# Building the gate tables of a PEER expert layer: one comparison for both tables on VectorE, and the gates multiplied in on GpSimd

## The chip, the cores and the metric

The kernel runs on one core of a Trainium2 chip. The metric is the device time of one execution in microseconds (us). An execution has five engines that run side by side and meet at semaphores: TensorE (PE, with its weight loads PEld), VectorE (DVE), ScalarE (ACT), GpSimd (POOL) and SyncE (SP), which here only issues transfers.

## The reference, cut to what matters

The kernel computes two layers of a backbone for 128 context tokens and 512 latent tokens, all in float32. Each layer ends in a PEER expert mixer. Every token has 8 heads, each head picks 16 pairs (i1, i2) of 128 x 128 experts with a softmax gate, so a token has 128 selections:

```python
v1, i1 = lax.top_k(s1, PEER_TOPK)
v2, i2 = lax.top_k(s2, PEER_TOPK)
...
idx = jnp.take_along_axis(cidx, pos, axis=-1)          # i1 * 128 + i2
gates = jax.nn.softmax(best, axis=-1).astype(h.dtype)
...
act = jax.nn.gelu(jnp.einsum('td,ted->te', xb, u_tab[ib])) * gb
return jnp.einsum('te,ted->td', act, v_tab[ib])
```

For three of the five tiles of 128 tokens (384 tokens) the kernel computes this densely over all 16,384 experts, and needs a dense table of gates: for each token a 128 x 128 matrix that holds the gate at (i1, i2) and zero elsewhere.

## The kernel before, in words

The program is a row of stages, each a block with a barrier of all engines at its end: load, modulation, the RWKV and Fourier layer, `peer` for layer 0, the Hyena layer, `peer` for layer 1, store. `peer` itself is `norm_modulate`, `peer_route` (top-16 and gates), `peer_dense_gates` (the change is here), `peer_experts` and `add_and_norm`. Nothing of one stage's engine work runs beside that of another.

`peer_dense_gates` gets `selT`: for each selection (partition) and each of 384 tokens the first index (row 0), the second index (row 1) and the gate (row 2). Tokens go in 96 groups of 4 (`QT`). A group k uses slot `k % 4` of the buffer `hot` and of the PSUM banks 0 to 3. In a slot, `hot[:, u, 1]` holds four one-hot tables of the second index, `hot[:, u, 0]` four one-hot tables of the first index times the gate, each 128 selections x 128 keys.

- VectorE makes table 1 with one `tensor_tensor` of 512 elements per partition (L604, `is_equal` of `selT` row 1 and `iota`), and table 0 with four `tensor_scalar` of 128 (L608), in which the comparison and the product with the gate are one instruction with two per-partition scalars. The 96 groups are written out; from the fifth on, the first instruction of a group waits until TensorE has finished the group four before (`pg_mm`).
- TensorE waits for the tables (`pg_hot`) and for a free bank (`pg_sb`), and does four float32 matmuls of 128x128 (L620), which the trace shows as eight.
- ScalarE copies the bank into `gates_sb`, 512 elements per partition (L632).
- SyncE stores 8,192 KB to memory after each 32 groups (L639), three times. The block ends when the last store has landed.
- GpSimd has no work in this stage but clearing semaphores at its end (L60 to L64).

The order on each engine is the order in the code: there is no planner.

Of the kernel before, what the change touches and what calls it, by code (L numbers as in the profile page):

```python
# [7 lines left out]
ALU = mybir.AluOpType  # L8
# [5 lines left out]
P = 128  # L14
# [52 lines left out]
def sems(ctx, nc, *names):  # L67

    s = {n: ctx.enter_context(nc.semaphore(f"{n}_{nc.next_id()}")) for n in names}
    ctx.callback(clear, nc, s)  # L70
    return s


def buf(ctx, nc, name, *shape, dtype=F32):
    return ctx.enter_context(nc.sbuf_tensor(f"{name}_{nc.next_id()}", list(shape), dtype))
# [275 lines left out]
PH, NKEY, TOPK = 8, 128, 16  # L351
# [232 lines left out]
def peer_dense_gates(nc, m, selT):  # L584


    QT = 4
    TBLS = 4
    GROUPS = TB // QT
    BLOCKS = NDT  # L590
    with ExitStack() as ctx:
        hot = buf(ctx, nc, "hot", P, TBLS, 2, QT, NKEY)
        G = [buf(ctx, nc, f"gates_sb{i}", P, NKEY, TB) for i in range(2)]
        s = sems(ctx, nc, "pg_hot", "pg_mm", "pg_sb", "pg_st0", "pg_st1")
        stored = [s["pg_st0"], s["pg_st1"]]
        table = [P, QT, NKEY]
        with nc.Block() as block:
            @block.vector
            def _(dve):
                for k in range(BLOCKS * GROUPS):  # L600
                    u = k % TBLS
                    if k >= TBLS:
                        dve.wait_ge(s["pg_mm"], k + 1)
                    dve.tensor_tensor(hot[:, u, 1], selT[:, 1, k * QT:(k + 1) * QT].unsqueeze(2).broadcast_to(table),  # L604
                                      m.iota[:, :].unsqueeze(1).broadcast_to(table), ALU.is_equal)
                    for q in range(QT):
                        t = k * QT + q
                        ins = dve.tensor_scalar(hot[:, u, 0, q, :], m.iota[:, :], selT[:, 0, t:t + 1], selT[:, 2, t:t + 1], ALU.is_equal, ALU.mult)  # L608
                    ins.then_inc(s["pg_hot"], 1)

            @block.tensor
            def _(pe):
                pe.sem_inc(s["pg_mm"], TBLS)
                with pe.Fori(0, BLOCKS * GROUPS // TBLS) as r:
                    for u in range(TBLS):
                        k = TBLS * r + u
                        pe.wait_ge(s["pg_hot"], k + 1)
                        pe.wait_ge(s["pg_sb"], k + 1)
                        for q in range(QT):
                            mm = pe.matmul(m.bank[u][:, q * P:(q + 1) * P], hot[:, u, 1, q, :], hot[:, u, 0, q, :], start=True, stop=True)  # L620
                        mm.then_inc(s["pg_mm"], 1)

            @block.scalar
            def _(act):
                act.sem_inc(s["pg_sb"], TBLS)
                for b in range(BLOCKS):
                    if b >= 2:
                        act.wait_ge(stored[b % 2], 16 * (b // 2))
                    with act.Fori(0, GROUPS // TBLS) as r:
                        for u in range(TBLS):  # L630
                            act.wait_ge(s["pg_mm"], TBLS * r + (b * GROUPS + u + 1 + TBLS))
                            act.activation(G[b % 2][:, :, bass.ds(r * 16 + 4 * u, 4)].rearrange("p i t -> p t i"),  # L632
                                           m.bank[u][:, :].rearrange("p (t i) -> p t i", t=4), ACT.Copy).then_inc(s["pg_sb"], 1)

            @block.sync
            def _(sp):
                for b in range(BLOCKS):
                    sp.wait_ge(s["pg_sb"], (b + 1) * GROUPS + TBLS)
                    sp.dma_start(m.gates[:, :, T0 + b * TB:T0 + (b + 1) * TB].rearrange("a i t -> i a t"), G[b % 2][:, :, :]).then_inc(stored[b % 2], 16)  # L639
                for b in range(BLOCKS - 2, BLOCKS):  # L640
                    sp.wait_ge(stored[b % 2], 16 * (b // 2 + 1))
# [215 lines left out]
def peer(nc, m, layer):  # L857
    with ExitStack() as rows:
        R = Shared()
        R.h = buf(rows, nc, "rows_h", P, NSP, D)  # L860
        R.idx = buf(rows, nc, "rows_idx", P, NSP, PH * TOPK, dtype=U32)
        R.gate = buf(rows, nc, "rows_gate", P, NSP, PH * TOPK)
        with ExitStack() as ctx:
            selT = buf(ctx, nc, "selT", P, 3, TD)
            with ExitStack() as inner:
                S = Shared()
                S.wq = buf(inner, nc, "wq", P, SIDES, KD, P)
                S.keys = buf(inner, nc, "keys", P, SIDES, NKEY)
                S.qT = buf(inner, nc, "qT", P, 2, P)
                s = sems(inner, nc, "ps_keys", "ps_w0", "ps_w1", "ps_w2", "ps_w3")  # L870

                def load_queries(sp):
                    for n in range(SIDES):
                        sp.dma_start(S.wq[:, n], m.i["peer_wq"][layer, n]).then_inc(s[f"ps_w{n // 4}"], 16)
                        if n == 0:
                            sp.dma_start(S.keys[:, :, :], m.i["peer_k"][layer]).then_inc(s["ps_keys"], 16)

                norm_modulate(nc, m, layer, 1, prefetch=load_queries)
                peer_route(nc, m, layer, S, s, selT, R)
            peer_dense_gates(nc, m, selT)  # L880
        R.y = buf(rows, nc, "rows_y", P, NSP, D)
        peer_experts(nc, m, layer, R)
        add_and_norm(nc, m, layer, 1, y=lambda t, h: R.y[:, t, h * BANK:(h + 1) * BANK] if t < NSP else m.bank[2 + 2 * (t - NSP) + h][:, :])
# [1195 lines left out]
```

## Time and profile before

| | us |
|---|---|
| median of 3 runs (5609.91 to 5612.98) | 5610.12 |
| the profiled execution | 5610.12 |
| its span in the trace | 5608.3 |
| TensorE busy | 4504.1 (80%) |
| VectorE busy | 3735.5 (67%) |
| GpSimd busy | 1933.1 (34%) |
| ScalarE busy | 1529.2 (27%) |

The span is the time from the first to the last instruction; the rest of the execution's time, 1.8 us, lies around it. Busy time is summed over stages with quite different limits, so the shares say nothing of the stage that is changed; it runs twice, from 2022.5 to 2212.7 us of the span and from 4265.4 to 4455.5 us. Start times are the ones to trust in it: on VectorE the spans of neighbours overlap, since a span begins when the instruction is taken up.

### The profile page before, as it was taken

The page shows a single profiled execution, that of the slowest core. Times are in us where ns is not written, and L with a number is a line of the kernel's source. Part 1 is how long each engine was busy: PE and PEld are TensorE (multiplying, and loading weights), DVE is VectorE, ACT ScalarE, POOL GpSimd, SP SyncE. Part 2 cuts the span into 40 slices and gives each one's busy share as a digit, 9 for nine tenths or more (in the row PEclk, how much of TensorE's full clock was granted, in tenths as well). Part 3 has the DMA queues.
Part 4 walks back from the last instruction along what each step waited for, and adds up shares of the span by engine and source line. Part 5 has one row for each costly group of instructions (what it writes and reads, how often), then busy time and mean ns, then how long its engine had stood idle before and what let it go on. Part 6 is the DMA issues. An engine that isn't in the chain of part 4 may idle for free. (4 is left out here: it accounts for less than half of the span.)

```text
span 5608.3 us, 71780 instructions
## 1 busy us (share of the span) xinstructions
PE 4504.1 (80%) x24898; PEld 3740.3 (67%) x24898; DVE 3735.5 (67%) x7416; ACT 1529.2 (27%) x2454; POOL 1933.1 (34%) x1556
## 2 busy tenths in 40 slices
PE   3678869679678945999999948877894499999995
PEld 0357758558565934999999945433583499999994
DVE  1143453543523986999999973342398699999997
ACT  0122313222121234333333321110123433333332
POOL 0021312313211320566666640000132056666664
PEclk8879879788789978999999979978997899999997
DMA  9110000000011016999999951101101699999995
GB/s 392 43 56 14 2 14 1 14 14 1 2 59 74 1 52 191 400 398 406 404 399 405 403 196 57 49 27 56 77 1 53 185 400 397 406 404 395 407 406 221
DMA packets 382998, 1049.15 MB, mean 187 GB/s; under 512 B 36647, under 2 KB 168999, under 8 KB 376616
## 3 DMA queue, kind: packets, MB, share of 16 engines
q0 software_dynamic: 147456, 536.94, 24.3%
q1 hardware_dynamic: 235368, 509.88, 24.3%
q8 instruction: 111, 1.82, 0.1%
q14 instruction: 63, 0.52, 0.0%
HBM read 990.62 MB, written 56.07 MB: 187 GB/s over the span
## 5 line engine op out<-in xcount | busy, mean ns | idle before, releaser
L728 PE MATMUL bank<-h_parts,u_parts 128*128 128x384 f32 x6144 | 1116.1, 336 | 97.5 <-DVE u_parts L803 97.5
L728 PEld LDWEIGHTS bank<-h_parts,u_parts 128*128 128x128 f32 x6144 | 1082.3, 188 | 117.3 <-issue 97.8
L738 PE MATMUL bank<-v_parts,gg_parts 128*128 128x512 f32 x4608 | 1095.7, 391 | 0.0
L700 POOL DMA_INDIRECT u_rows<-in_u_rows,rows_idx x512 | 697.5, 1362 | 1087.5 <-DVE dots L807 599.0
L738 PEld LDWEIGHTS bank<-v_parts,gg_parts 128*128 128x128 f32 x4608 | 861.2, 188 | 170.6
L813 DVE SCALAR_TENSOR_TENSOR rows_y<-v_rows,row_scale,rows_y 128x1024 f32<-128x1024 f32 x512 | 661.5, 1293 | 29.0 <-DMA v_rows<-in_peer_v,rows_idx 14.6
L706 POOL DMA_INDIRECT v_rows<-in_peer_v,rows_idx x512 | 608.4, 1188 | 168.2 <-issue 149.3
L807 DVE CUSTOM_DVE_ANT_0 u_rows<-u_rows,rows_h 128x1024 f32<-128x1024 f32 x512 | 622.5, 1216 | 0.0
L803 DVE TENSOR_TENSOR u_parts<-hT,u_parts 128x1024 fp32r<-128x1024 f32 x260 | 317.0, 1219 | 69.4 <-ACT u_parts L776 41.5
L1228 POOL TENSOR_TENSOR early<-region,lmask 128x256 f32<-128x256 f32 x300 | 212.3, 729 | 362.2 <-DVE region L1467 199.1
L302 POOL TENSOR_TENSOR x<-x,gb 128x1024 f32<-128x1024 f32 x20 | 46.9, 2346 | 831.6 <-ACT x L295 831.6
L429 PE MATMUL bank<-hT,wq 128*128 128x128 f32 x2560 | 310.5, 275 | 4.5 <-PEq L60 4.5
L842 DVE TENSOR_TENSOR v_parts<-v_in,v_parts 128x1024 fp32r<-128x1024 f32 x256 | 311.7, 1218 | 0.0
L772 ACT ACTIVATE ge<-bank 128x384 f32<-128x384 f32 x256 | 126.1, 493 | 669.8 <-PE bank L728 543.0
L620 PE MATMUL bank<-hot 128*128 128x128 f32 x1536 | 226.2, 292 | 94.8 <-DVE hot L608 94.8
L429 PEld LDWEIGHTS bank<-hT,wq 128*128 128x128 f32 x2560 | 297.9, 192 | 4.9 <-issue 4.9
L779 ACT ACTIVATE gg_parts<-gg 128x384 fp32r<-128x384 f32 x256 | 134.7, 526 | 587.1 <-PE bank L738 481.8
L620 PEld LDWEIGHTS bank<-hot 128*128 128x128 f32 x1536 | 190.9, 196 | 130.5 <-DVE hot L608 130.4
L776 ACT ACTIVATE u_parts<-hT 128x1024 fp32r<-128x1024 f32 x256 | 269.9, 1054 | 0.0
L781 ACT ACTIVATE v_parts<-v_in 128x1024 fp32r<-128x1024 f32 x256 | 268.0, 1047 | 0.0
L1481 DVE TENSOR_TENSOR XT<-XT,bank 128x512 f32<-128x512 f32 x150 | 103.2, 688 | 237.9 <-PE bank L1304 237.9
L608 DVE TENSOR_SCALAR hot<-iota,selT 128x128 f32<-128x128 f32 x768 | 251.1, 540 | 0.0
(302 smaller groups left out, 6584.9 us busy)
## 6 DMA issues: line engine op xcount, KB each, us to landing
hT<-in_peer_u SPq DMA_DIRECT2D x260, 512.0 KB
v_in<-in_peer_v SPq DMA_DIRECT2D x256, 512.0 KB
w_modt<-in_w_mod SPq DMA_DIRECT2D x24, 2048.0 KB
gates<-gates_sb SPq DMA_DIRECT2D x6, 8192.0 KB, 30.4
g_in<-gates SPq DMA_DIRECT2D x256, 192.0 KB
wq<-in_peer_wq SPq DMA_DIRECT2D x32, 512.0 KB, 12.4
w_hy<-in_hy_w_in SPq DMA_DIRECT2D x9, 1536.0 KB, 6.4
w_rkv<-in_w_rkv SPq DMA_DIRECT2D x6, 1536.0 KB, 6.8
```

Source lines behind the costliest of these rows:

```text
L429: mm = pe.matmul(m.bank[n % 2][:, 0:P], S.wq[:, n, k, :], m.hT[:, k, t * P:(t + 1) * P], start=(k == 0), stop=(k == KD - 1))
L620: mm = pe.matmul(m.bank[u][:, q * P:(q + 1) * P], hot[:, u, 1, q, :], hot[:, u, 0, q, :], start=True, stop=True)
L700: pool.indirect_dma_start(ug[n % GR][:, :], None, m.i["u_rows"], bass.IndirectOffsetOnAxis(ap=R.idx[:, n % 2, n // 2:n // 2 + 1], axis=0)) ...
L706: pool.indirect_dma_start(vg[n % GR][:, :], None, v_table, bass.IndirectOffsetOnAxis(ap=R.idx[:, n % 2, n // 2:n // 2 + 1], axis=0)).then_ ...
L728: mm = pe.matmul(m.bank[j % 2][:, 0:TD], us[:, j % 2, a, k, :], hs[:, b, k, :], start=(k == 0 and i == 0), stop=(k == KD - 1 and i == 2))
L738: mm = pe.matmul(yb[t][c][:, :], gs[:, j, a, t * P:(t + 1) * P], vs[:, j % 2, b, c * BANK:(c + 1) * BANK], start=(first and i == 0), stop= ...
L776: act.activation(us[:, j % 2, 0], u_in[:, (j + 2) % 4], ACT.Copy).then_inc(s["pe_uhi"], 1)
L781: act.activation(vs[:, j % 2, 0], v_in[:, j], ACT.Copy).then_inc(s["pe_vhi"], 1)
L803: dve.tensor_tensor(us[:, slot, 1], u_in[:, raw], us[:, slot, 0].bitcast(F32), ALU.subtract).then_inc(s["pe_ulo"], 1)
L807: dve.tensor_tensor_reduce(ug[q % GR][:, :], ug[q % GR][:, :], R.h[:, q % 2, :], 1.0, 0.0, ALU.mult, ALU.add, sd[:, q:q + 1]).then_inc(s[" ...
L813: dve.scalar_tensor_tensor(R.y[:, q % 2, :], vg[q % GR][:, :], sa[:, q:q + 1], R.y[:, q % 2, :], ALU.mult, ALU.add).then_inc(s["pe_axpy"], 1)
L842: dve.tensor_tensor(vs[:, j % 2, 1], v_in[:, j], vs[:, j % 2, 0].bitcast(F32), ALU.subtract).then_inc(s["pe_vlo"], 1)
```

## The change

In each group VectorE makes both one-hot tables with one `tensor_tensor` of 1,024 elements per partition, without the gate. GpSimd then multiplies table 0 by the gate in place, 512 elements per partition, and TensorE waits for GpSimd (`pg_gated`) where it waited for VectorE. Both new loops run over registers (24 turns of four groups), where VectorE's groups were written out.

```diff
-        s = sems(ctx, nc, "pg_hot", "pg_mm", "pg_sb", "pg_st0", "pg_st1")
+        s = sems(ctx, nc, "pg_hot", "pg_gated", "pg_mm", "pg_sb", "pg_st0", "pg_st1")
...
-        table = [P, QT, NKEY]
+        table = [P, 2, QT, NKEY]
...
-                for k in range(BLOCKS * GROUPS):
-                    u = k % TBLS
-                    if k >= TBLS:
+                with dve.Fori(0, BLOCKS * GROUPS // TBLS) as r:
+                    for u in range(TBLS):
+                        k = TBLS * r + u
                         dve.wait_ge(s["pg_mm"], k + 1)
-                    dve.tensor_tensor(hot[:, u, 1], selT[:, 1, k * QT:(k + 1) * QT].unsqueeze(2).broadcast_to(table),
-                                      m.iota[:, :].unsqueeze(1).broadcast_to(table), ALU.is_equal)
-                    for q in range(QT):
-                        t = k * QT + q
-                        ins = dve.tensor_scalar(hot[:, u, 0, q, :], m.iota[:, :], selT[:, 0, t:t + 1], selT[:, 2, t:t + 1], ALU.is_equal, ALU.mult)
-                    ins.then_inc(s["pg_hot"], 1)
+                        dve.tensor_tensor(hot[:, u], selT[:, 0:2, bass.ds(k * QT, QT)].unsqueeze(3).broadcast_to(table),
+                                          m.iota[:, :].unsqueeze(1).unsqueeze(1).broadcast_to(table), ALU.is_equal).then_inc(s["pg_hot"], 1)
+
+            @block.gpsimd
+            def _(pool):
+                with pool.Fori(0, BLOCKS * GROUPS // TBLS) as r:
+                    for u in range(TBLS):
+                        k = TBLS * r + u
+                        pool.wait_ge(s["pg_hot"], k + 1)
+                        pool.tensor_tensor(hot[:, u, 0], hot[:, u, 0], selT[:, 2, bass.ds(k * QT, QT)].unsqueeze(2).broadcast_to([P, QT, NKEY]),
+                                           ALU.mult).then_inc(s["pg_gated"], 1)
...
-                        pe.wait_ge(s["pg_hot"], k + 1)
+                        pe.wait_ge(s["pg_gated"], k + 1)
```

On VectorE, at the start of the stage, this stood in a row before (L598 is the stage's entry; `pg_mm` counts TensorE's finished groups; "128x512" is partitions x elements of the output):

```order
L598 UNCONDITIONAL_BRANCH [waits barrier_Pool_Activation_PE_DVE_SP_release]
L604 TENSOR_TENSOR hot<-selT,iota 128x512
L608 TENSOR_SCALAR hot<-iota,selT 128x128 x4
...
L604 TENSOR_TENSOR hot<-selT,iota 128x512 [waits pg_mm_7442]
L608 TENSOR_SCALAR hot<-iota,selT 128x128 x4
```

and this stands there now, the body of the loop cut after its first group:

```order
L598 UNCONDITIONAL_BRANCH [waits barrier_Pool_Activation_PE_DVE_SP_release]
L600 UNCONDITIONAL_BRANCH
L600 ISA
L604 ISA [waits pg_mm_7443]
L604 TENSOR_TENSOR hot<-selT,iota 128x1024
L603 REGISTER_ALU
```

The four `tensor_scalar` of a group are gone, and the `tensor_tensor` has doubled. On GpSimd, in the same stage, there was nothing between two barriers but the clearing of semaphores (L64), and then the first gather of the next stage:

```order
L61 UNCONDITIONAL_BRANCH [waits barrier_Pool_Activation_PE_DVE_SP_gather]
L64 ISA x5
L60 UNCONDITIONAL_BRANCH
L695 UNCONDITIONAL_BRANCH [waits barrier_Pool_Activation_PE_DVE_SP_gather]
L700 DMA u_rows_8270<-in_u_rows,rows_idx 128x1024
```

Now its loop stands ahead of them (`pg_hot` counts VectorE's finished tables):

```order
L607 UNCONDITIONAL_BRANCH [waits barrier_Pool_Activation_PE_DVE_SP_gather]
L609 UNCONDITIONAL_BRANCH
L609 ISA
L613 ISA [waits pg_hot_7441]
L613 TENSOR_TENSOR hot<-hot,selT 128x512
L612 REGISTER_ALU
```

GpSimd has become a link between VectorE and TensorE, with one instruction per group.

## Rows read from the trace of the kernel before

**Rows 1.** Groups of instructions, 2015 to 2360 us; busy and mean, idle before and releaser.
```profile
L608 DVE TENSOR_SCALAR hot<-iota,selT 128x128 f32<-128x128 f32 x384 | 126.3, 547 | 0.0
L620 PE MATMUL bank<-hot 128*128 128x128 f32 x768 | 113.1, 293 | 47.4 <-DVE hot L608 47.4
L632 ACT ACTIVATE gates_sb<-bank 128x512 f32 x96 | 102.4, 1067 | 58.7 <-PE bank L620 58.6
L604 DVE TENSOR_TENSOR hot<-selT,iota 128x512 f32<-128x512 f32 x96 | 85.4, 890 | 17.0 <-PEq L60 17.0
```

**Rows 2.** Timeline of the stage: start, length in us, engine and line, idle before.
```profile
2022.52 0.69 DVE L604 TENSOR_TENSOR hot<-selT,iota 128x512 f32<-128x512 f32 x1 [16.96 <-PEq L60]
...
2033.89 0.72 DVE L604 TENSOR_TENSOR hot<-selT,iota 128x512 f32<-128x512 f32 x1
2034.06 1.16 PE L620 MATMUL bank<-hot 128*128 128x128 f32 x8 [0.47 <-DVE hot L608]
2034.49 1.14 DVE L608 TENSOR_SCALAR hot<-iota,selT 128x128 f32<-128x128 f32 x4
...
2176.77 1.09 DVE L604 TENSOR_TENSOR hot<-selT,iota 128x512 f32<-128x512 f32 x1
```

**Rows 3.** Engines' busy time in the steady part, then TensorE's granted clock, DMA.
```profile
2032.00:2178.00 146.00, 103.78 (x718) 86.83 (x719) 146.00 (x451) 96.17 (x91) 0.00 (x0) 1.00 0.41 115
```

**Rows 4.** Timeline of the stage's beginning on TensorE and of its end.
```profile
2024.30 7.67 PE L620 MATMUL bank<-hot 128*128 128x128 f32 x40 [4.67 <-DVE hot L608]
...
2181.28 0.37 SPq L639 DMA_DIRECT2D gates<-gates_sb  x1
2212.70 3.42 ACT L756 ACTIVATE h_parts<-hT 128x384 fp32r<-128x384 f32 x8 [31.45 <-PEq L60]
```

**Rows 5.** VectorE comparing 2,048 elements (timeline, routing) and its 1,024-element subtraction (page).
```profile
1996.35 4.49 DVE L577 TENSOR_TENSOR eq<-ab,iota 128x2048 f32<-128x2048 f32 x2
...
L803 DVE TENSOR_TENSOR u_parts<-hT,u_parts 128x1024 fp32r<-128x1024 f32 x260 | 317.0, 1219 | 69.4 <-ACT u_parts L776 41.5
```

**Rows 6.** Groups of instructions on GpSimd, whole span: its products and sums.
```profile
L1228 POOL TENSOR_TENSOR early<-region,lmask 128x256 f32<-128x256 f32 x300 | 212.3, 729 | 362.2 <-DVE region L1467 199.1 <-PE bank L1296 163.0
L510 POOL TENSOR_TENSOR eq<-eq,idxf 128x2048 f32<-128x2048 f32 x20 | 90.0, 4522 | 326.3 <-DVE eq L577 326.3
L302 POOL TENSOR_TENSOR x<-x,gb 128x1024 f32<-128x1024 f32 x20 | 46.9, 2346 | 831.6 <-ACT x L295 831.6
L516 POOL TENSOR_TENSOR eq<-eq 128x512 f32<-128x512 f32 x10 | 10.4, 1041 | 0.8
```

**Rows 7.** One line of VectorE: its six instructions (min/median/max ns), and the timeline around one.
```profile
L537 DVE TENSOR_TENSOR sel<-gatex,norm x6: 291/293/4252, 1946.1 to 4244.1; 128x128 f32<-128x128 f32 x6
...
2000.92 8.99 POOL L510 TENSOR_TENSOR eq<-eq,idxf 128x2048 f32<-128x2048 f32 x2 [19.58 <-DVE eq L577]
2001.31 4.25 DVE L537 TENSOR_TENSOR sel<-gatex,norm 128x128 f32<-128x128 f32 x1
```

**Rows 8.** Timeline of GpSimd in the RWKV stage.
```profile
333.02 1.98 POOL L1213 TENSOR_TENSOR region<-region,rkv 128x640 f32<-128x640 f32 x1
335.08 1.99 POOL L1216 TENSOR_TENSOR bonus<-region 128x640 f32<-128x640 f32 x1
337.15 1.99 POOL L1218 TENSOR_TENSOR bonus<-bonus,rkv 128x640 f32<-128x640 f32 x1
```

**Rows 9.** Timeline of VectorE in that stretch, and a little later with GpSimd idle.
```profile
333.64 2.04 DVE L1452 TENSOR_TENSOR region<-region,early 128x640 f32<-128x640 f32 x1
335.61 2.15 DVE L1456 TENSOR_TENSOR early<-early,kk 128x640 f32<-128x640 f32 x1
337.79 2.04 DVE L1459 TENSOR_TENSOR x<-kk,region 128x640 f32<-128x640 f32 x1
...
348.58 0.82 DVE L1459 TENSOR_TENSOR x<-rkv,region 128x640 f32<-128x640 f32 x1
349.31 0.82 DVE L1460 TENSOR_TENSOR BK<-early,region 128x640 f32<-128x640 f32 x1
```

## The prediction, made before the changed kernel was run

> **What bounds the kernel now.** I read the page's costliest groups for the lines of the changed stage, then the groups of the stage alone, then its timeline, and last every place where GpSimd and VectorE work at once. The stage is bound by VectorE. In the groups of the stage, TensorE's matmuls and ScalarE's copies sit idle for VectorE's L608 and for TensorE, while VectorE's two lines have no idle time but 17.0 us ahead of the first [rows 1]. In the steady part VectorE is busy for all of 146 us, TensorE for 104, ScalarE for 96, GpSimd for nothing [rows 3]. The pace has to be read from starts, as VectorE's spans overlap (the busy times of its two lines would give 2.2 us a group): L604 starts first at 2022.52 and last at 2176.77, which is 95 steps of 1.624 us [rows 2]. Of one step L604 holds 0.60 (2033.89 to 2034.49) and the four L608 hold the other 1.02. TensorE does its eight matmuls in 1.16 us and then waits 0.47 for L608. ScalarE's copy takes 1.07 us [rows 1]. After the last group comes the store of 8 MB, issued at 2181.28; the next stage starts at 2212.70 [rows 4]. The stage occurs twice, with 96 groups each, so each 0.01 us a group is worth 1.92 us.
>
> **The change part by part.**
>
> VectorE's side by itself. Removed are four L608 and one 512-element L604, 1.624 us a group. Added is one comparison of 1,024 elements. The trace has the same operation with 2,048 elements: two of L577 take 4.49 us, so 2.25 each, and half is 1.12. The subtraction L803 of 1,024 elements takes 1.22 with everything in it [rows 5]. Alone, VectorE would need 1.10 to 1.22 us a group.
>
> GpSimd's side by itself. Its product of 512 elements is bounded by rows 6. Below: L516, 512 elements, 1.04 us. Above: from L1228 (256 elements, 0.73) to L302 (1,024 elements, 2.35) an element costs 2.11 ns, so 512 cost 0.73 + 256 x 2.11 ns = 1.27. A quarter of L510, the same product with one operand spread out, is 1.13. So 1.04 to 1.27.
>
> Each is well below 1.624. If they ran side by side the stage would get shorter. Whether they do is the question on which the sign hangs, and the trace has an answer in two places.
>
> The first is L537, a VectorE product of 128 elements with both inputs in SBUF. Its median is 0.293 us and its longest 4.252. One of the long ones starts at 2001.31, while GpSimd's L510 runs from 2000.92; the first of the two takes 4.52 [rows 6], so it ends at 2005.44, and L537 ends at 2005.56 [rows 7]. VectorE had stood still until GpSimd let go. The second is a stretch of the RWKV stage, where both engines have several 640-element `tensor_tensor` in a row. With GpSimd idle, VectorE starts one such each 0.73 us (348.58, 349.31). Beside GpSimd, its three start at 333.64, 335.61 and 337.79, 2.07 us apart on average [rows 9], and GpSimd's three start at 333.02, 335.08 and 337.15, also 2.07 apart [rows 8]. They alternate: VectorE's end at 335.68, 337.76 and 339.83, each 0.68 or 0.69 us after GpSimd's (335.00, 337.07, 339.14), which is about the work of 640 elements; and GpSimd's end 1.39 and 1.38 us after VectorE's. So 0.69 + 1.38 = 2.07: two `tensor_tensor` that read SBUF cost the sum of the two, not the larger. The new stage is just that pair, 96 times over.
>
> Scaled by elements: VectorE 0.69 x 1024/640 = 1.10 us, GpSimd 1.38 x 512/640 = 1.10 us. If GpSimd has a fixed part, 512 elements cost a bit more: 1.38 less 128 elements at 2.11 ns is 1.11. I add 0.02 on VectorE for the half of L577 (1.12) and take 2.23 us a group. The change is 2.23 - 1.624 = 0.606 us, times 192 is +116 us. The bounds of the two parts give 1.10 + 1.04 = 2.14 (+99 us) and 1.22 + 1.27 = 2.49 (+166 us).
>
> By the Trainium skill, page "SBUF — State Buffer", section "Who interferes with whom", a VectorE instruction with two SBUF inputs contends with a GpSimd instruction that reads SBUF, and whichever issues first has the shared ports for its whole instruction. Taken at its word, the full length of each counts, which is the upper sum of 2.49 us; the rows of the alternating stretch say that only the time of the elements does, 2.07 us where the lengths alone (0.82, and 0.73 + 384 x 2.11 ns = 1.54 for GpSimd by rows 6) would be 2.36. I go by the rows. The page also says that a VectorE instruction with one SBUF input outside the two-port modes doesn't contend; the four L608 run with GpSimd idle, so no row here bears on them.
>
> Waits. What is queued behind VectorE's new wait is only its next comparison. Four slots let VectorE run ahead; one group needs 1.12 + 1.10 + TensorE's 1.16 and some handoffs, with each waiting for the other's turn at most once 5.6 us, less than four groups at 2.23 (8.9). So TensorE never ends a wait last, and whenever one of the two is held by a semaphore, the other has work. The register instructions of the loops lie on one engine while the other computes: I cost them at nothing; uncovered, 0.1 us a group would be +19 us.
>
> TensorE and ScalarE stay off the path: 1.16 and 1.07 against 2.23. At the lower clock, as when the stage begins, TensorE did 40 matmuls (five groups) in 7.67 us, 1.53 a group [rows 4], still less. The stage is at clock 1.00 now [rows 3]; should half-idle TensorE fall to its lower level, it costs nothing. Stores: 32 groups will last 71 us and a store 31, so only the last one is bare, as now. The head and tail of the stage each gain one link (GpSimd after VectorE for the first and last group), some 1.2 us a stage; one more semaphore to clear: together +3 us.
>
> Sum: the profiled execution took 5610.12 us, 1.8 more than its span, and equals the median, so 5610 + 116 + 3 = 5729.
>
> **The rivals.**
>
> *Side by side.* The two engines don't hold each other up here. Then the pace is the slowest of VectorE 1.12, GpSimd 1.13, TensorE 1.16 and ScalarE 1.07, at best 1.17 with handoffs: (1.17 - 1.624) x 192 = -87 us, 5526 us. For it: the trace has no pair of exactly these shapes, with one operand spread out on each side. Against it: L510 has a spread-out operand and did hold L537 up [rows 7].
>
> *Partly side by side.* The hold covers only a part of GpSimd's instruction, and the pace is near what it is now, 1.6 to 1.65: within some 5 us of before, 5612. Against it: in the alternating stretch nothing of either is hidden.
>
> *The sum and the handoffs.* Each change of hands and each register loop costs time in which nobody works, or the engines fall into a round trip with one group in flight: 1.12 + 1.10 + 1.16 is 3.4 in the worst case; with 0.2 us for two changes of hands and 0.2 for the loops 2.63, or +193 us, 5806 us. For it: neither engine has such a loop in the trace. Against it: alternation in the RWKV stretch is without gaps, and there are four slots.
>
> **How the numbers follow.** The sum with small handoffs: 0.82; with its own range 5700 to 5785 from the bounds 2.14 and 2.49 and the margin of the loops. Sum and handoffs: 0.09. Side by side: 0.06. Partly: 0.03. The range 5695 to 5790 holds nearly all of the first and little of the others. Within 0.2%, about what a measurement of this kernel can tell from no change (11 us), lies only a part of the third: 0.02. Faster: 0.07. Slower: 0.91.
>
> **What would show it.** In the groups of the stage, VectorE's 1,024-element comparison should have a mean near 2.1 us, since its time includes the wait for GpSimd, or GpSimd's product one near 2, and starts on either should be 2.23 us apart. TensorE's idle time should be put down to GpSimd's L613 with about 1.07 us a group. From the first comparison to the last should be 212 us a stage instead of 154. Each step has its own sign: comparisons 1.1 us long and 1.2 us apart would mean side by side; starts 2.6 us apart with short instructions and gaps would mean that loops or handoffs cost. All other stages should keep their lengths to a microsecond or so. The forecast is wrong if what holds in the RWKV stretch doesn't hold for operands that are spread out, or if in a long run one engine can slip in while the other's instruction is in progress.

## The result, and the profile after

The changed kernel takes 5676.59 us (median of 4 runs, 5672.23 to 5678.41) against 5611.26 us for the kernel before on the same chip: a ratio of 1.0115 with a 95% interval of 1.0098 to 1.0133. It is slower, as forecast, but by 65 us where 119 were forecast, and lies below the range of 5695 to 5790. The profiled execution took 5675.5 us with a span of 5673.7, so the spans differ by 65.4.

The difference comes from the two stages that build the gate tables. From the first comparison to ScalarE's first instruction of the next stage, the first stage took 2022.52 to 2212.70 [rows 2, 4], which is 190.18 us, and takes 2019.94 to 2244.08 now, 224.14 us: +33.96. The second went from 190.2 to 224.4 us, +34.3. The three other pieces of the program, before, between and after, differ by -2.6, +2.7 and -2.9 us. Such pieces move by as much between runs: the first comparison of the stage starts anywhere from 2018.9 to 2024.1 us in the traces of this case.

The groups of instructions of the changed stage, 2015 to 2400 us, answer to [rows 1]:

```profile
L613 POOL TENSOR_TENSOR hot<-hot,selT 128x512 f32<-128x512 f32 x96 | 188.8, 2004 | 5.5 <-DVE hot L604 5.5
L604 DVE TENSOR_TENSOR hot<-selT,iota 128x1024 f32<-128x1024 f32 x96 | 188.4, 2038 | 17.1 <-PEq L618 17.1
L625 PE MATMUL bank<-hot 128*128 128x128 f32 x768 | 132.9, 328 | 61.6 <-POOL hot L613 60.8
...
L637 ACT ACTIVATE gates_sb<-bank 128x512 f32 x96 | 101.7, 1060 | 93.5 <-PE bank L625 92.7
```

VectorE and GpSimd look busy all the time, each with instructions of 2.0 us. TensorE now waits for GpSimd's L613. The line's own view gives the shortest beside the median, and the first and last start (VectorE's of the first stage, then GpSimd's of both):

```profile
L604 DVE TENSOR_TENSOR hot<-selT,iota x96: 1220/2055/2060, 2019.9 to 2206.3; 128x1024 f32<-128x1024 f32 x96
L613 POOL TENSOR_TENSOR hot<-hot,selT x192: 1033/2016/2019, 2021.4 to 4488.7; 128x512 f32<-128x512 f32 x192
```

The shortest comparison takes 1.22 us: it is one of the first two of a stage, which run before GpSimd has anything to do. The shortest product takes 1.03: it is the last of a stage, when VectorE has finished. All others contain a wait for the other engine. From the first start to the last, 2019.94 to 2206.27, are 95 steps of 1.961 us, where it had been 1.624 [rows 2]: 0.338 x 192 = 65 us. In steady running the step is 1.98 us (1.979 from VectorE's 20th start to its 90th); the mean is a little less, since the first two steps of VectorE are 1.14 us long. The timeline of two of TensorE's groups:

```profile
2060.86 1.16 PE L625 MATMUL bank<-hot 128*128 128x128 f32 x8 [0.82 <-POOL hot L613]
2062.14 1.06 ACT L637 ACTIVATE gates_sb<-bank 128x512 f32 x1 [0.93 <-PE bank L625]
...
2062.84 1.16 PE L625 MATMUL bank<-hot 128*128 128x128 f32 x8 [0.82 <-POOL hot L613]
```

Four instructions in a row, each taken from a narrow window of the timeline, show the turns. A start says only when an instruction was taken up, so ends are read, as the forecast did in the RWKV stretch:

```profile
2103.36 2.06 DVE L604 TENSOR_TENSOR hot<-selT,iota 128x1024 f32<-128x1024 f32 x1
2104.30 2.02 POOL L613 TENSOR_TENSOR hot<-hot,selT 128x512 f32<-128x512 f32 x1
2105.34 2.06 DVE L604 TENSOR_TENSOR hot<-selT,iota 128x1024 f32<-128x1024 f32 x1
2106.28 2.02 POOL L613 TENSOR_TENSOR hot<-hot,selT 128x512 f32<-128x512 f32 x1
```

VectorE's end at 2105.42 and 2107.40, GpSimd's at 2106.32 and 2108.30. GpSimd's end comes 0.90 us after VectorE's, and VectorE's 1.08 us after GpSimd's. These two spans are called the turns, or holds, below; they add up to the 1.98 us of a group.

The steady part as a window, which answers to [rows 3], and the end of the stage, which answers to [rows 4]:

```profile
2032.00:2200.00 168.00, 116.84 (x680) 99.29 (x680) 168.00 (x86) 90.11 (x85) 168.00 (x86) 0.87 0.36 100
```

```profile
2212.61 0.37 SPq L644 DMA_DIRECT2D gates<-gates_sb  x1
2244.08 3.42 ACT L761 ACTIVATE h_parts<-hT 128x384 fp32r<-128x384 f32 x8 [31.50 <-PEq L60]
```

TensorE's granted clock, the last number but two, has gone from 1.00 to 0.87 of full speed: part of the time it is at the lower of its two levels, 1.2 GHz. TensorE now sits idle for 0.82 us between its groups, where it was 0.47 [rows 2]; that this is why the clock falls was not tested. It costs nothing: where the clock is low, the eight weight loads of a group take 1.71 us (0.97 else), and the next group still starts 1.98 us later:

```profile
2043.04 1.71 PEld L625 LDWEIGHTS bank<-hot 128*128 128x128 f32 x8 [0.30 <-POOL hot L613]
2045.02 0.97 PEld L625 LDWEIGHTS bank<-hot 128*128 128x128 f32 x8 [0.27 <-POOL hot L613]
```

The last store still stands bare, 31.5 us.

### The profile page after: what moved, and what is told of

The parts are those of the page before. It is cut to its first block and busy times, and to the rows that moved or that the text cites. A ratio compares the mean times of both kernels' runs of the same rounds, so it can differ in the third digit from the quotient of the medians.

```text
span 5673.7 us, 72170 instructions
## 1 busy us (share of the span) xinstructions
PE 4543.2 (80%) x24898; PEld 3776.1 (67%) x24898; DVE 3798.9 (67%) x6648; ACT 1526.8 (27%) x2454; POOL 2309.9 (41%) x1748
## 5 line engine op out<-in xcount | busy, mean ns | idle before, releaser
L604 DVE TENSOR_TENSOR hot<-selT,iota 128x1024 f32<-128x1024 f32 x192 | 376.8, 2038 | 34.2 <-PEq L618 34.2
L613 POOL TENSOR_TENSOR hot<-hot,selT 128x512 f32<-128x512 f32 x192 | 377.7, 2004 | 10.9 <-DVE hot L604 10.9
L625 PE MATMUL bank<-hot 128*128 128x128 f32 x1536 | 266.1, 328 | 123.0 <-POOL hot L613 121.5
L625 PEld LDWEIGHTS bank<-hot 128*128 128x128 f32 x1536 | 226.9, 227 | 162.6 <-POOL hot L613 162.6
```

Source lines behind the costliest of these rows:

```text
L604: dve.tensor_tensor(hot[:, u], selT[:, 0:2, bass.ds(k * QT, QT)].unsqueeze(3).broadcast_to(table), m.iota[:, :].unsqueeze(1).unsqueeze(1). ...
L613: pool.tensor_tensor(hot[:, u, 0], hot[:, u, 0], selT[:, 2, bass.ds(k * QT, QT)].unsqueeze(2).broadcast_to([P, QT, NKEY]), ALU.mult).then_ ...
```

## The experiments

Theory A is the forecast's mechanism: VectorE's comparison with two inputs in SBUF and GpSimd's product that reads SBUF can't run at the same time, and a group costs the sum of what the two need of the shared way to SBUF. Against it stands B, a round trip: 1.98 us is the length of a chain through VectorE, GpSimd, TensorE and back, with waiting shown as long instructions. Both fit the profile after. "Pace" below is the first to the last start of VectorE's first line in the first stage, over 95 steps. Most experiments are a single run; five runs of e1 lie 11 us apart from lowest to highest, so the pace and the lengths in each trace weigh more than a few us of its time.

**e1: the same work, with one of VectorE's inputs in PSUM.**

```diff
+                dve.tensor_copy(m.bank[4][:, 0:NKEY], m.iota[:, :]).then_inc(s["pg_io"], 1)
+                dve.wait_ge(s["pg_io"], 1)
                 with dve.Fori(0, BLOCKS * GROUPS // TBLS) as r:
...
-                                          m.iota[:, :].unsqueeze(1).unsqueeze(1).broadcast_to(table), ALU.is_equal).then_inc(s["pg_hot"], 1)
+                                          m.bank[4][:, 0:NKEY].unsqueeze(1).unsqueeze(1).broadcast_to(table), ALU.is_equal).then_inc(s["pg_hot"], 1)
```

> The changed kernel, with the key numbers 0 to 127 copied once to a PSUM bank that this stage doesn't use, and the comparison on VectorE reading them there, so that it has one input in SBUF and not two. Instructions, semaphores and slots are else the same. Theory A (turns: the two engines' SBUF reads exclude each other, 1.98 us a group is the sum of 1.09 and 0.89): the turns end, comparison near 1.22 us and product near 1.03 long, pace near 1.15 us a group, time near 5611 - (1.624 - 1.15) x 192 = 5520 us. Rival B (round trip: 1.98 us is the length of the chain VectorE, GpSimd, TensorE and back over the slots and semaphores, and both spans contain waiting for it): nothing changes, 1.98 us a group, near 5676 us.

Measured: 5517.33 us (median of 5 runs, 5514.05 to 5525.5) against 5609.39 for the kernel before, a ratio of 0.984 with an interval of 0.9827 to 0.9854. The groups of the stage, 2015 to 2500 us:

```profile
L627 PE MATMUL bank<-hot 128*128 128x128 f32 x768 | 109.6, 291 | 5.9 <-POOL hot L615 5.9
L606 DVE TENSOR_TENSOR hot<-selT,bank 128x1024 f32<-128x1024 f32 x96 | 109.0, 1210 | 1.1 <-PE bank L627 0.5 <-DVE bank L600 0.3
L639 ACT ACTIVATE gates_sb<-bank 128x512 f32 x96 | 102.5, 1074 | 13.7 <-PE bank L627 8.5
L615 POOL TENSOR_TENSOR hot<-hot,selT 128x512 f32<-128x512 f32 x96 | 100.0, 1041 | 15.3 <-DVE hot L606 7.1
```

The comparison takes 1.21 us and the product 1.04, together, with the same semaphores and slots; the pace is 1.142 us. B named 1.98 for this run, and falls: the chain through the engines is the same, and only the place of one input has changed. This version is faster than both kernels: VectorE has next to no idle time, and TensorE and ScalarE are nearly as full.

**e2: the changed kernel without the product** (the gates are not applied). GpSimd's block is taken out, and TensorE waits for VectorE:

```diff
-            @block.gpsimd
...
-                        pe.wait_ge(s["pg_gated"], k + 1)
+                        pe.wait_ge(s["pg_hot"], k + 1)
```

> The changed kernel without GpSimd's product: the gates are not applied, and TensorE waits for VectorE. Theory A: VectorE's comparison costs 1.10 to 1.14 us a group alone, and the pace is that or TensorE's 1.16: near 1.15 us, some 5520 us. Rival B: about the same, since a link is gone; this run gives VectorE's own term.

Measured: 5518.72 us, one run.

```profile
L604 DVE TENSOR_TENSOR hot<-selT,iota x96: 1212/1215/1225, 2023.5 to 2131.6; 128x1024 f32<-128x1024 f32 x96
```

The comparison with both inputs in SBUF takes the same 1.215 us when GpSimd is idle, pace 1.138. So the PSUM input of e1 didn't make the comparison faster by itself; it only took it out of GpSimd's way. And e1 costs no more than this run, which has no product: in e1 GpSimd is hidden whole. Both theories had named some 5520 us for this run, so it doesn't choose between them.

**e3, e4 and e8: why the product held VectorE for 0.89 us and not 1.10.** The forecast had scaled it from products of 640 elements in which both operands are read element by element. The changed kernel's is of 512 elements, with a gate that stands for 128 elements in a row ("spread" below; "dense" is an operand read element by element). Three runs part the form from the size; in all of them values other than the gates are multiplied in.

```diff
-                        pool.tensor_tensor(hot[:, u, 0], hot[:, u, 0], selT[:, 2, bass.ds(k * QT, QT)].unsqueeze(2).broadcast_to([P, QT, NKEY]),
-                                           ALU.mult).then_inc(s["pg_gated"], 1)
+                        pool.tensor_tensor(hot[:, u, 0], hot[:, u, 0], hot[:, u, 1], ALU.mult).then_inc(s["pg_gated"], 1)
```

That is e3. In e4 the first 640 elements of the slot are multiplied by `selT[:, 2, 0:QT + 1]`, spread over 128 elements each; in e8 by 640 elements of `selT` read one by one.

> The changed kernel with GpSimd multiplying table 0 by table 1, 512 elements each, both read element by element, in place of the gate that is read once per 128 elements; the gates are not applied. The question is why the product held VectorE 0.89 us where 1.10 was forecast from products with two densely read operands. Theory C (operand): a spread operand is cheaper, so here the hold is near 1.10 us and the pace near 2.2 us a group, near 5717 us. Rival D (size: 512 elements cost less per element than 640, whatever the operand): pace stays at 1.98, near 5676 us.

> The changed kernel with GpSimd multiplying 640 elements of the slot in place, by an operand of five values read once per 128 elements; values differ from the gates. Theory C (operand): 0.89 x 640/512 = 1.11 us of hold, pace near 2.20 us, near 5720 us. Rival D (size): the hold is that of the 640-element products of the RWKV stretch, 1.38, pace near 2.47 us, near 5771 us.

> The changed kernel with GpSimd multiplying 640 elements of the slot in place by 640 others, both read element by element, the shape of the RWKV stretch on which the forecast was scaled; the gates are not applied. Theory C (operand): 1.09 + 1.38 = 2.47 us a group, near 5773 us, which would close the account: forecast from 640 dense, ran 512 spread. If the product's time in the RWKV stretch had been set by something else of that stage, near 2.2 us, 5720 us.

Measured, one run each: 5719.09, 5714.53 and 5770.73 us. The product's line in e3, in e4 and in e8 (shortest, median, longest):

```profile
L613 POOL TENSOR_TENSOR hot<-hot x192: 1267/2245/2255, 2024.3 to 4530.9; 128x512 f32<-128x512 f32 x192
```

```profile
L613 POOL TENSOR_TENSOR hot<-hot,selT x192: 1251/2233/2237, 2022.3 to 4527.4; 128x640 f32<-128x640 f32 x192
```

```profile
L613 POOL TENSOR_TENSOR hot<-hot,selT x192: 1542/2515/2522, 2024.5 to 4584.2; 128x640 f32<-128x640 f32 x192
```

The comparison's line in the same three runs gives the paces 2.184, 2.173 and 2.450 us; of e8 it reads:

```profile
L604 DVE TENSOR_TENSOR hot<-selT,iota x96: 1218/2555/2559, 2023.2 to 2255.9; 128x1024 f32<-128x1024 f32 x96
```

Theory C (operand) named 5717, near 5720 and near 5773, D (size) 5676 and 5771 for the first two: D falls twice. The shortest product of each line, again the last of a stage, is the unhindered one: 512 elements take 1.27 us with the dense operand and not 1.03, and the kernel with it costs 5719, where C had named 5717.

**e5 and e6: half of each part.** In e5 VectorE compares 512 elements a group (the other table is set to ones once); in e6 GpSimd multiplies 256 (half of the gates are not applied). The edits of e5, then of e6:

```diff
-                        dve.tensor_tensor(hot[:, u], selT[:, 0:2, bass.ds(k * QT, QT)].unsqueeze(3).broadcast_to(table),
+                        dve.tensor_tensor(hot[:, u, 0], selT[:, 0, bass.ds(k * QT, QT)].unsqueeze(2).broadcast_to([P, QT, NKEY]),
```

```diff
-                        pool.tensor_tensor(hot[:, u, 0], hot[:, u, 0], selT[:, 2, bass.ds(k * QT, QT)].unsqueeze(2).broadcast_to([P, QT, NKEY]),
+                        pool.tensor_tensor(hot[:, u, 0, 0:2], hot[:, u, 0, 0:2], selT[:, 2, bass.ds(k * QT, 2)].unsqueeze(2).broadcast_to([P, 2, NKEY]),
```

> The changed kernel with VectorE comparing only 512 elements a group (the table that GpSimd multiplies); the other table is set to ones once, so the gates are not the reference's. It tests that VectorE's term of the sum goes with its elements. Theory A (turns): 0.56 + 0.89 = 1.45 us a group, 5611 - (1.624 - 1.45) x 192 = near 5578 us. If instead GpSimd's product had slowed by some fixed factor beside VectorE (span 2.0 us for 1.03), the pace would stay near 2.0 us, near 5676 us.

> The changed kernel with GpSimd multiplying only two of the four tokens of a group, 256 elements; half of the gates are not applied. Theory A with the cheap spread operand: 1.09 + 0.45 = 1.54 us a group, near 5595 us. If the hold has a large fixed part, as the forecast with 2.11 ns an element implied (1.10 for 512, so 0.56 for 256), 1.65 us, near 5616 us.

Measured: 5578.0 and 5593.65 us, one run each, against 5578 and 5595. The comparison's line in e5, then in e6:

```profile
L606 DVE TENSOR_TENSOR hot<-selT,iota x96: 687/1523/1529, 2023.0 to 2158.7; 128x512 f32<-128x512 f32 x96
```

```profile
L604 DVE TENSOR_TENSOR hot<-selT,iota x96: 1221/1628/1637, 2020.7 to 2167.3; 128x1024 f32<-128x1024 f32 x96
```

The paces are 1.428 and 1.543 us. Each part counts by its own elements, and neither slows by a factor: a comparison of 512 that takes 0.69 us alone shows 1.52, more than the full one alone.

The ends of the instructions, read as above from the 20th group to the 90th, give the two turns of every run by themselves (us; the lengths are the shortest of the run, unhindered):

| run | VectorE's turn | its length alone | GpSimd's turn | its length alone | sum of turns |
|---|---|---|---|---|---|
| changed kernel | 1.08 | 1.22 | 0.90 | 1.03 | 1.98 |
| e3, dense 512 | 1.08 | 1.22 | 1.13 | 1.27 | 2.21 |
| e4, spread 640 | 1.08 | 1.22 | 1.12 | 1.25 | 2.20 |
| e8, dense 640 | 1.08 | 1.22 | 1.40 | 1.54 | 2.48 |
| e5, compares 512 | 0.55 | 0.69 | 0.90 | 1.03 | 1.45 |
| e6, multiplies 256 | 1.08 | 1.22 | 0.47 | 0.61 | 1.55 |

An edit on one engine moves that engine's turn and leaves the other's where it was. Every turn is 0.13 to 0.15 us shorter than the instruction alone.

**e7 and e9: the product moved, nothing merged.** VectorE keeps the written-out groups of the kernel before, and only the gate leaves its four `tensor_scalar`; GpSimd multiplies as in the changed kernel:

```diff
-                        ins = dve.tensor_scalar(hot[:, u, 0, q, :], m.iota[:, :], selT[:, 0, t:t + 1], selT[:, 2, t:t + 1], ALU.is_equal, ALU.mult)
+                        ins = dve.tensor_scalar(hot[:, u, 0, q, :], m.iota[:, :], selT[:, 0, t:t + 1], None, ALU.is_equal)
```

> The kernel before with the gate taken out of VectorE's four tensor_scalar (comparison alone) and applied by GpSimd as in the changed kernel: the product is moved, and nothing on VectorE is merged. It asks whether tensor_scalar with one SBUF input takes turns with GpSimd too. If it does (theory F): 0.56 + 1.02 + 0.89 = 2.47 us a group, near 5773 us. If it doesn't (theory G): GpSimd's 0.89 us fit beside the four tensor_scalar, and the pace is between VectorE's own 1.62 and 1.75 us, 5611 to 5635 us.

Measured: 5709.49 us, one run, which neither theory had named; the pace is 2.16. So e9 takes GpSimd's product out of e7.

> The kernel of the run with the product moved and nothing merged, but without GpSimd's product (the gates are not applied; TensorE waits for VectorE). That run paced 2.17 us a group, between the 2.47 of theory F (turns with tensor_scalar too) and the 1.62 to 1.75 of theory G (none). Theory F with a cheaper tensor_scalar: a comparison without the product costs less than 0.255 us, and VectorE alone takes 2.17 - 0.89 = 1.28 us a group here or somewhat more, near 5545 to 5560 us. Theory G: VectorE alone keeps 1.62 us a group (5611 us), and the extra 0.55 us of that run came from only the tensor_tensor taking turns with the product.

Measured: 5563.43 us, one run, a little above the 5545 to 5560 of theory F and far from the 5611 of theory G; the pace is 1.386. The timeline of VectorE in e9, and that of VectorE and GpSimd in e7:

```profile
2061.50 0.67 DVE L604 TENSOR_TENSOR hot<-selT,iota 128x512 f32<-128x512 f32 x1
2062.10 0.86 DVE L608 TENSOR_SCALAR hot<-iota,selT 128x128 f32<-128x128 f32 x4
2062.88 0.68 DVE L604 TENSOR_TENSOR hot<-selT,iota 128x512 f32<-128x512 f32 x1
```

```profile
2061.67 0.68 DVE L604 TENSOR_TENSOR hot<-selT,iota 128x512 f32<-128x512 f32 x1
2061.93 1.31 POOL L617 TENSOR_TENSOR hot<-hot,selT 128x512 f32<-128x512 f32 x1 [0.85 <-DVE hot L608]
2062.27 1.65 DVE L608 TENSOR_SCALAR hot<-iota,selT 128x128 f32<-128x128 f32 x4
...
2063.84 0.68 DVE L604 TENSOR_TENSOR hot<-selT,iota 128x512 f32<-128x512 f32 x1
```

Alone, a group takes 1.39 us (0.60 for L604 and 0.78 for the four L608); with the product 2.17 in steady running. The product costs 0.78 us of VectorE's time, less than its turn of 0.90. L604 has ended at 2062.35, and for the other 0.9 us of the product's 1.31, until 2063.24, only a `tensor_scalar` is due on VectorE. Its line in e7, and the first of the four L608 above by itself, show that it is the one blocked:

```profile
L608 DVE TENSOR_SCALAR hot<-iota,selT x768: 272/275/1066, 2019.7 to 4523.0; 128x128 f32<-128x128 f32 x192
```

```profile
2062.27 1.06 DVE L608 TENSOR_SCALAR hot<-iota,selT 128x128 f32<-128x128 f32 x1
```

Its median is 0.275 us and its longest 1.066, which is 0.79 more. The long one is the first of the four, in 190 of the 192 groups. The product ends 0.90 us after L604, its usual turn, and the waiting L608 0.08 us after the product, where in e9 it ends 0.20 us after L604: 0.90 + 0.08 - 0.20 is the 0.78. So turns are taken with this `tensor_scalar` as well (theory F). Both my numbers for e7 were wrong. Of the 0.30 us between theory F's 2.47 and the measured 2.17, 0.24 are the `tensor_scalar`, which without its second operation costs 0.20 us a step (0.78/4) and not the 0.255 of before; the 0.12 by which a blocked one ends sooner make up the rest. By the Trainium skill, page "SBUF — State Buffer", section "Who interferes with whom", `tensor_scalar` can enter a mode in which it uses both ports and then contends with GpSimd; e7 and e9 agree, with 0.78 us a group. This `tensor_scalar` also reads a per-partition scalar from SBUF beside `iota`, and no run parts the two: which of them makes it contend is not shown.

## Why the forecast had the sign and missed the size

- *What bounds the kernel now* held: VectorE at 1.624 us a group, and the 192 groups' new pace makes up the difference.
- *Alternation* held, and decided the sign. The rows of the RWKV stretch [rows 8, 9] were the right ones to read it from: e1 ends it by moving one input, with the rest of each group unchanged.
- *VectorE's term*, 1.10 us and 0.02 added, nearly held: its turn is 1.08 us.
- *GpSimd's term is the step that failed*: "GpSimd 1.38 x 512/640 = 1.10 us". The product as it is made here holds for 0.90 us. Scaling by elements from [rows 8] left out that there both operands are dense. For a dense one 1.10 was nearly right: e3 has 1.13. The lower bound, 1.04 from the 512-element L516 [rows 6], was wrong too: I took the full length of an instruction for the floor of its hold, though the RWKV stretch shows that the hold is shorter than the length (1.38 against the 1.54 that the forecast itself had from rows 6, and that e8 gives for it alone). So the range began too high. With 0.14 taken off, L516 would have given 0.90. That would have been luck: L516 is an addition with no spread operand, of another form.
- *L510, "the same product with one operand spread out"*, was misread. In its code, `iv[:, :, side, :].unsqueeze(2)`, the 16 values that are used again are read one by one in each turn, and not each held for a run of elements as the gate is. Its 4.52 us for 2,048 elements are 2.2 ns an element, the price of a dense product. So no row of before had the form of the new product.
- *The size of the miss*: between the forecast's +119 and the +65 of the profiled executions are 54 us. 48 of them are the pace, 1.979 for 2.23: 38 for GpSimd's turn (0.90 for 1.10), 8 for VectorE's (1.08 for 1.12), 2 for rounding the sum up. 3 are the head and tail, and 3 the other stages.
- *The full length of each*, as the Trainium skill has it (page "SBUF — State Buffer", section "Who interferes with whom"): 1.22 + 1.03 = 2.25 us; measured 1.98. The measurement decides: each turn is about 0.14 us shorter than the instruction's own time. The rows had said so, and the forecast followed them on this point in its sum, but not in its lower bound.
- *TensorE, ScalarE, loops and stores at nothing* held. TensorE's fall to its lower clock in part of the stage, priced at nothing, cost nothing.
- *Head and tail, +3 us*, were not needed: 96 steps of the steady pace (1.979 - 1.624) are 34.1 us, and the stages grew by 34.0 and 34.3. From the last comparison's start to the next stage it does take 1.9 us longer, but the first two comparisons, which meet no product, give that back.
- *All other stages to a microsecond or so* was too narrow: they moved by up to 2.9 us, which is what such pieces do between runs.
- *The rivals*: side by side didn't happen here, but 5526 us was its price, and e1, which makes it happen, has 5517. Sum and handoffs with 2.63 us didn't occur: e5, e6 and e8 come out within 3 us of sums without any handoff, and the turns are shorter than the instructions alone.

Not shown: why a turn falls 0.14 us short of an instruction's length (it may be the time in which it does not read SBUF). The runs show its size only.

## What to carry to other kernels

Before moving part of VectorE's work to GpSimd, look at where VectorE's inputs lie: with two in SBUF (or a `tensor_scalar` of the kind here) the two engines add up, and the move pays only if GpSimd's turn is shorter than what VectorE is rid of. Here VectorE went from 1.62 to 1.08 us a group, and GpSimd's turn is 0.90. Putting one small constant operand into an unused PSUM bank turned 1.2% slower into 1.6% faster. When a price is scaled from another row, scale from the same form of operands, and read the hold from the ends of alternating instructions; in this case it was the length less 0.14 us.

## What the runs showed of the hardware that I had not expected

- In the changed stage, a GpSimd product with one operand spread over 128 elements is cheaper than a dense one. Unhindered, 512 elements took 1.03 us spread and 1.27 dense, 640 took 1.25 and 1.54. Per element that is (1.251 - 1.033)/128 = 1.70 ns spread and (1.542 - 1.267)/128 = 2.15 ns dense. By the Trainium skill, page "GPSIMD Engine Reference", section "3.1 Elementwise — side-by-side cycle accounting", a `tensor_tensor` costs about 2.6 cycles an element at 1.2 GHz, an estimate of 2.17 ns: the dense runs agree, and the spread ones are below it.
- Spread or dense isn't the whole rule. In the kernel before, L516 adds 2 of every 16 elements to the next 2, and L517 one to its neighbour, with no spread operand: 512 take 1.04 us [rows 6] and 256 take 0.62, nearly as little as the spread products (1.03, and 0.61 in e6). L516 on 4 of every 16, 1,024 elements, takes 2.32 us, the price of a dense one. No run shows what sets this. The two lines that [rows 6] lacks:

```profile
L516 POOL TENSOR_TENSOR eq<-eq 128x1024 f32<-128x1024 f32 x10 | 23.2, 2324 | 0.8
L517 POOL TENSOR_TENSOR sel<-eq 128x256 f32<-128x256 f32 x10 | 6.2, 623 | 0.8
```

- VectorE's comparison as `tensor_scalar` of 128 elements costs 0.20 us a step with one operation and 0.255 with two and a second per-partition scalar (e9 against [rows 2]).
- VectorE's `tensor_tensor` takes as long with one input in PSUM (1.210 us) as with both in SBUF (1.215).
